# Fourteen more weight chunks by seven part products, with the sums and joins written anew

## The chip, the cores and the metric

One Trainium2 chip, one of its cores. The time is device microseconds of one execution of the whole program; several executions are timed and their median is given. A profile is one execution taken by the hardware profiler; its times are counted from the start of its span.

## The reference, cut to what matters

Four layers run on 256 tokens of width 1024, all in float32. The first two (the "first block") are a feed-forward part, a mixer and a second feed-forward part. The mixer multiplies the normed tokens by one wide matrix and splits the result:

```python
u = rms_norm(h, mix_norm[l])
(z_s, xbc, dt_s, qkv, z_d, b_d, a_d, gate_s, gate_d) = jnp.split(u @ w_in[l], split_points, axis=-1)
y_s = mamba2_branch(z_s, xbc, dt_s, ...)        # scan over 32 heads; y * silu(z), normed by groups
y_d = deltanet_branch(qkv, z_d, b_d, a_d, ...)  # qkv = silu(conv of 4 taps(qkv)), then q, k, v
merged = sigmoid(gate_s) * (y_s @ ssm_w_branch[l]) + sigmoid(gate_d) * (y_d @ dn_w_branch[l])
h = h + merged @ w_out[l]
```

The last two layers (the "second block") are a retention and convolution mixer, a cross attention, and a feed-forward part whose "up" product goes through a short convolution before it is gated.

## The kernel before, in words

**Chunks.** All weights stream from memory through a ring of three slots of 1 MB (`stream`, issued on SP's queue). A slot, a chunk, is 16 tiles of 128 x 128 and gives 256 output features for 256 tokens. A chunk c is loaded once chunk c - 2 has begun on TensorE (PE).

**Two ways to multiply a chunk.** Plain (`product`): 16 matmuls with 256 moving columns. By seven part products (`Tensor.seven`): the 2 x 2 blocks of the weights and of the tokens are combined by sums, as in Winograd's form of Strassen's algorithm, and seven products of half the size (4 matmuls of 128 columns each, 28 in all) replace eight. They are named B11, B21, B22, T1 to T4 and collect in two PSUM banks, X and Y. Four sums of weights are needed, made on VectorE (DVE) by `weights_by_dve` (for xbc's five chunks on GpSimd by `weights_by_pool`); four sums of tokens are made once for a stage (`sums_by_dve`, for the feed-forward outputs `feed_by_pool`). The order on PE, where the sums of tokens are old, is B11, B21, T4, then, once the first weight sums are there, T3, T2 (X is complete), T1, B22 (Y is complete). ScalarE (ACT) copies one quarter of X (`part_by_act`, L1006), and `join` on DVE adds the quarters into two tiles of output.

**Which chunks.** Every feed-forward chunk and many others go by seven. In the first block's mixer xbc has five of twelve (`BY_SEVEN`), z six of eight (`Z_SEVEN`) and q, k, v six of twelve, the odd ones (`Q_SEVEN`).

**The order around the change.** The scan of the first branch runs in 19 steps (`BESIDE`). Steps 0 to 6 carry the chunks z1 to z7, steps 7 to 18 the chunks q0 to q11. In a step PE multiplies the chunk, then makes the scan's y product (steps 0 to 15; it needs DVE's `mix` of that step), then spreads decays for three steps on. In steps 7, 11, 15 and 18 it also sums squares over partitions (`y_norm`), for which DVE must have added the squares (`y_summed`, at the end of steps 5, 9, 13 and 17). After step 18 come four z_d chunks and one gate chunk, all by seven.

DVE works through each step in a fixed order, and it takes no instruction out of turn: the weight sums of the **next** chunk if it goes by seven, the join of this chunk if it does, `mix` of the next step (L1705), the convolution of a q, k, v chunk (three taps for two tiles, L1616, once ACT has made the first tap, L1265 or L1279), `y_out` (L1712, L1714), for z chunks the gate (L1688), and in steps 5, 9, 13 and 17 the addition of squares (L1744, L1746). For a plain q, k, v chunk ACT copies the bank to the padded tile (L1273) and DVE has neither sums nor join.

**The start.** The tokens x come in four quarters on ACT's queue, behind the gain of the first norm; the first chunk's rows come in four pieces on SP's. The first two chunks are multiplied plain with raw tokens (`opening`). The second chunk is loaded once the last quarter of x has landed, and its load is one transfer; behind it on SP stand the constants, parameters and the third chunk.

Of the kernel before, what the change touches and what calls it, by code (L numbers as in the profile page):

```python
# [15 lines left out]
P = 128  # L16
# [128 lines left out]
class Sems:  # L145


    def __init__(self, ctx, nc):
# [137 lines left out]
class Lane:  # L286


    def __init__(self, e, sems, banks):
        self.e, self.sems, self.banks, self.seen = e, sems, banks, Seen()  # L290


class Tensor:
# [46 lines left out]
    def chunk(self):  # L340

        c, at = divmod(self.used, TILES)
        assert at == 0
        self.used += TILES
        if c:
            self.e.wait_ge(self.sems.w_loaded[c % RING], 16 * loads(c))
        self.fresh = c > 0
        return self.ring[:, c % RING, :]
# [39 lines left out]
    def seven(self, sums, f, at, X, Y, acts, first, last, ready=None, new=False, by_token=False):  # L388


        e, sems = self.e, self.sems
        if at[0] == 0:
            self.whole = self.chunk()
        a = lambda i, g: self.whole[:, (i * GROUPS + g) * P:(i * GROUPS + g + 1) * P]
        s = lambda i, g: sums.s[:, f % 2, i - 1, g * P:(g + 1) * P]
        part = lambda bank, i: bank[:, i * P:(i + 1) * P]

        def product(bank, i, weights, what, fresh, stop):
            for g in at:
                if ready:  # L400
                    ready(what, g)

                both = (acts(what, g), weights(g)) if by_token else (weights(g), acts(what, g))
                ins = self.mm(part(bank, i), *both, fresh and g == at[0], stop and g == at[-1])
            return ins

        def summed(n):
            e.wait_ge(sems.sum_by_pool if f in BY_POOL else sems.sum_by_dve, 4 * SUMMED[f] + n)

        def finished(ins):  # L410
            if last:
                ins.then_inc(sems.bulk_done, 1)

        product(X, 0, lambda g: a(0, g), "B11", first, False)
        product(X, 1, lambda g: a(1, g), "B21", False, False)
        if ready:
            summed(4)
            product(Y, 2, lambda g: s(4, g), "B22", first, False)
            if new:
                product(Y, 1, lambda g: s(1, g), "T1", False, False)  # L420
            product(X, 2, lambda g: s(2, g), "T2", False, False)
            finished(product(X, 3, lambda g: s(3, g), "T3", False, last))
            if not new:
                product(Y, 1, lambda g: s(1, g), "T1", False, False)
            finished(product(Y, 0, lambda g: a(3, g), "T4", False, last))
        else:
            product(Y, 0, lambda g: a(3, g), "T4", first, False)
            summed(2)
            product(X, 3, lambda g: s(3, g), "T3", False, False)
            summed(3)  # L430
            finished(product(X, 2, lambda g: s(2, g), "T2", False, last))
            product(Y, 1, lambda g: s(1, g), "T1", False, False)
            summed(4)
            finished(product(Y, 2, lambda g: s(4, g), "B22", False, last))

    def opening(self, outs, done, n, again=False):

# [7 lines left out]
        for at, (m, k) in enumerate(order):  # L445
            if at == SUM_AT[n] and n and not again:
                self.square_sums(n)
                if n == CLOSE1 + 1:
                    self.square_sums(CLOSE1)
            if m == 0 and not again:  # L450
                e.wait_ge(sems.raw_ready, scaled(n) + k + 1)
            if n == 0 and not again and m == 0 and k % 2 == 0:
                e.wait_ge(sems.rows_loaded[k // 2], 16)
            i = m * KD + k

            ins = self.mm(outs[m], w[:, i * P:(i + 1) * P], raw[:, k, :], k == 0 and (m == 0 or done[0]), k == KD - 1 and done[m])
            if k == KD - 1 and done[m]:
                ins.then_inc(sems.bulk_done, 1)
# [100 lines left out]
def stream(e, sems, parts, ring, before):  # L559

    c = 0
    for dram, n in parts:
        for i in range(n):
            before(c)
            if c >= RING:
                e.wait_ge(sems.w_used, c - RING + 1)

            if c:
                e.dma_start(ring[:, c % RING, :], dram[i]).then_inc(sems.w_loaded[c % RING], 16)
            c += 1  # L570

# [469 lines left out]
def last_weights_by_dve(v, seven, ring, f):  # L1041
# [2 lines left out]
    w = ring[:, c % RING, :].rearrange("p (i n) -> p i n", i=4)  # L1044
    s = seven.s[:, f % 2]
    e.wait_ge(sems.sum_by_dve, 4 * SUMMED[f] + 3)
    e.tensor_tensor(s[:, 3, :], w[:, 1, :], s[:, 1, :], ALU.subtract).then_inc(sems.sum_by_dve, 1)  # L1047


def weights_by_dve(v, seven, ring, f, last=True):  # L1050
# [5 lines left out]
    if f >= 2:  # L1056

        e.wait_ge(sems.w_used, FAST[f - 2] + 1)
    e.tensor_tensor(s[:, 0, :], w[:, 2, :], w[:, 3, :], ALU.add).then_inc(sems.sum_by_dve, 1)  # L1059
    e.tensor_tensor(s[:, 2, :], w[:, 0, :], w[:, 2, :], ALU.subtract).then_inc(sems.sum_by_dve, 1)  # L1060
    e.wait_ge(sems.sum_by_dve, 4 * SUMMED[f] + 1)
    e.tensor_tensor(s[:, 1, :], s[:, 0, :], w[:, 0, :], ALU.subtract).then_inc(sems.sum_by_dve, 1)  # L1062
    if last:
        last_weights_by_dve(v, seven, ring, f)

# [1 line left out]
def weights_by_pool(g, seven, ring, f):  # L1067
# [8 lines left out]
    e.tensor_tensor(s[:, 0, :], w[:, 2, :], w[:, 3, :], ALU.add).then_inc(sems.sum_by_pool, 1)
    e.tensor_tensor(s[:, 2, :], w[:, 0, :], w[:, 2, :], ALU.subtract).then_inc(sems.sum_by_pool, 1)
    e.wait_ge(sems.sum_by_pool, 4 * SUMMED[f] + 1)
    e.tensor_tensor(s[:, 1, :], s[:, 0, :], w[:, 0, :], ALU.subtract).then_inc(sems.sum_by_pool, 1)
# [10 lines left out]
def sums_by_dve(v, x, seven, at):  # L1090
# [5 lines left out]
    e.tensor_tensor(tx[1], high[:, :, P:S], tx[0], ALU.subtract).then_inc(sems.tx_by_dve, 1)  # L1096
    e.wait_ge(sems.tx_by_dve, at + 2)
    e.tensor_tensor(tx[2], high[:, :, P:S], low[:, :, P:S], ALU.subtract).then_inc(sems.tx_by_dve, 1)
    e.tensor_tensor(tx[3], high[:, :, 0:P], tx[1], ALU.subtract).then_inc(sems.tx_by_dve, 1)


def join(v, seven, L, name, i, high=None, in_place=False, to=None):
# [7 lines left out]
    twice = lambda x: x.unsqueeze(1).to_broadcast([P, 2, P])  # L1110
    e.wait_ge(sems.part_copied, PARTS_FROM[L, name] + i + 1)

    e.tensor_tensor(quarter[:, 0:2, 0, :], twice(a), X[:, 1:3, :], ALU.add).then_inc(sems.dve_step, 1)  # L1113
    e.wait_ge(sems.dve_step, seen.up("dve_step"))
    e.tensor_tensor(w, u, X[:, 3, :], ALU.add).then_inc(sems.bulk_read_dve, 1)  # L1115
    e.wait_ge(sems.bulk_done, BULK.filled(L, name, (i, 1)))
    e.tensor_tensor(quarter[:, 0, 1, :], u, Y[:, 1, :], ALU.add).then_inc(sems.dve_step, 1)  # L1117
    e.wait_ge(sems.bulk_read_dve, BULK.read(L, name, (i, 0)))
    if in_place:

        high = c[:, 1, :]
        e.wait_ge(sems.dve_step, seen["dve_step"] + 1)
# [78 lines left out]
def feed_by_pool(g, m, L, job):  # L1201
# [3 lines left out]
    def hidden(k):  # L1205
# [317 lines left out]
def first_dve(v, m, m2, L, par, par_next, cst, ring, ones):  # L1523
# [1405 lines left out]
def program(nc, hT_d, memT_d, pos_d, p1, w1, p2, w2, cst_d, dmask_d, outT):  # L2929
    with ExitStack() as ctx:  # L2930
# [30 lines left out]
        with nc.Block() as block:  # L2961
# [206 lines left out]
```

## Time and profile before

| | us |
|---|---|
| median of 3 runs | 3204.95 (3203.97 to 3206.16) |
| the profiled execution, its own time | 3207.67 |
| its span | 3205.9 |
| PE busy | 3187.9 (99%) |
| DVE busy | 2350.6 (73%) |
| ACT busy | 665.5 (21%) |
| GpSimd busy | 274.5 (9%) |

Busy time is the time in which an engine has at least one instruction in work; matmuls are pipelined, so a busy PE need not be at its peak. Instructions of one engine overlap a little: where one lasts 0.68 us, the next may begin 0.60 us after it. A float32 matmul of the program is two matmul records in the trace, so a chunk by seven is 56 records and a plain one 32.

### The profile page before, as it was taken

How to read it: one execution, taken by the hardware profiler on the slowest of the kernel's cores; microseconds unless marked ns; L12 is line 12 of the kernel's file. 1: busy time of each engine (PE TensorE's matmuls, PEld its weight loads, DVE VectorE, ACT ScalarE, POOL GpSimd, SP SyncE). 2: the span in 40 equal slices, each digit the busy share in tenths (PEclk: the TensorE clock that was granted, in tenths of full speed). 3: DMA queues.
4: the chain of work that ended last, by engine and by line, in shares of the span. 5: the costliest groups of instructions: out<-in, count | busy, mean ns of one | idle time of the engine just before them, and what ended most of it. 6: DMA issues, size and time to landing. Idle time of an engine off the chain costs nothing.

```text
span 3205.9 us, 59487 instructions
## 1 busy us (share of the span) xinstructions
PE 3187.9 (99%) x25008; PEld 3034.8 (95%) x25008; DVE 2350.6 (73%) x5234; ACT 665.5 (21%) x1625; POOL 274.5 (9%) x339
## 2 busy tenths in 40 slices
PE   9999999999999999999999999999999999999998
PEld 9999999899999999998999999879999999889998
DVE  6657786276676577873867898877786988877885
ACT  1113433211111134332211111211211111212211
POOL 0202000001102020000011000300021000300031
PEclk9999999999999999999999999999999999999999
DMA  5544444344444444443544444344444445343453
GB/s 203 171 158 136 141 146 154 103 162 169 170 170 165 157 141 145 148 149 110 193 165 167 168 166 168 130 148 145 149 169 170 161 169 172 120 156 130 160 172 132
DMA packets 89643, 497.50 MB, mean 155 GB/s; under 512 B 25088, under 2 KB 29600, under 8 KB 30368
## 3 DMA queue, kind: packets, MB, share of 16 engines
q1 hardware_dynamic: 70608, 489.45, 44.8%
q10 hardware_dynamic: 18768, 4.25, 0.7%
q8 instruction: 197, 3.23, 0.4%
q14 instruction: 70, 0.57, 0.0%
HBM read 491.55 MB, written 2.11 MB: 154 GB/s over the span
## 4 chain that ended last, share of the span: by engine, by line
PE 94%; DVE 4%; ACT 1%; issue 0%; DMA 0%; ACTq 0%; DVEq 0%
PE bank L352 87%; DVE arena L1062 1%; DVE arena L1047 1%; DVE arena L1060 1%; PE bank L2063 1%; PE bank L2858 0%; PE bank L2117 0%; PE bank L2802 0%; PE bank L2839 0%; DVE arena L1059 0%; ACT arena L2425 0%; PE bank L2042 0%; DVE arena L2697 0%; DVE arena L2704 0%; PE bank L523 0%
## 5 line engine op out<-in xcount | busy, mean ns | idle before, releaser
L352 PE MATMUL bank<-arena 128*128 128x128 f32 x9240 | 1092.8, 275 | 2.6 <-DVE arena L1047 2.6
L352 PEld LDWEIGHTS bank<-arena 128*128 128x128 f32 x9240 | 1061.6, 192 | 3.4 <-DVE arena L1047 3.4
L352 PE MATMUL bank<-arena,ring 128*128 128x128 f32 (+1 forms) x6312 | 991.1, 310 | 2.4 <-DMA ring<-w 1.3
L352 PEld LDWEIGHTS bank<-arena,ring 128*128 128x128 f32 x6312 | 896.0, 192 | 59.6 <-issue 2.9
L352 PE MATMUL bank<-xT,ring 128*128 128x128 f32 (+1 forms) x5008 | 725.2, 300 | 0.3 <-DVE arena L1127 0.3
L352 PEld LDWEIGHTS bank<-xT,ring 128*128 128x128 f32 x5008 | 669.8, 192 | 31.0 <-issue 0.7
L1006 ACT ACTIVATE arena<-bank 128x128 f32<-128x128 f32 x311 | 85.9, 276 | 1105.3 <-PE bank L352 1099.5
L1059 DVE TENSOR_TENSOR arena<-ring 128x512 f32<-128x512 f32 x343 | 235.2, 686 | 107.1 <-PE bank L352 103.8
L1113 DVE TENSOR_TENSOR arena<-arena,bank 128x256 f32<-128x256 f32 x311 | 129.6, 417 | 220.0 <-ACT arena L1006 219.0
L352 PE MATMUL bank<-xT,arena 128*128 128x128 f32 x1928 | 255.6, 276 | 0.1
L1047 DVE TENSOR_TENSOR arena<-ring,arena 128x512 f32<-128x512 f32 x343 | 241.9, 705 | 11.5
L1062 DVE TENSOR_TENSOR arena<-arena,ring 128x512 f32<-128x512 f32 x343 | 242.9, 708 | 0.0
L1060 DVE TENSOR_TENSOR arena<-ring 128x512 f32<-128x512 f32 x343 | 241.0, 703 | 0.0
L352 PEld LDWEIGHTS bank<-xT,arena 128*128 128x128 f32 x1928 | 234.8, 192 | 1.6 <-DVE arena L1047 1.6
L2479 DVE SCALAR_TENSOR_TENSOR arena<-arena,par 128x256 f32<-128x256 f32 x480 | 204.2, 494 | 0.0
L1117 DVE TENSOR_TENSOR arena<-arena,bank 128x128 f32<-128x128 f32 x311 | 88.5, 284 | 131.0 <-PE bank L352 130.7
L1616 DVE SCALAR_TENSOR_TENSOR arena<-arena,par 128x256 f32<-128x256 f32 x288 | 138.2, 548 | 50.3 <-ACT arena L1279 34.8
L1208 POOL TENSOR_TENSOR arena<-arena 128x128 f32<-128x128 f32 x66 | 40.1, 607 | 1161.0 <-DVE arena L1138 651.9
L1124 DVE TENSOR_TENSOR arena<-arena,bank 128x256 f32<-128x256 f32 x311 | 129.3, 416 | 10.6
L2732 POOL TENSOR_TENSOR arena<-arena 128x512 f32<-128x512 f32 x10 | 44.9, 4494 | 661.1 <-ACT arena L2344 661.0
L1115 DVE TENSOR_TENSOR arena<-arena,bank 128x128 f32<-128x128 f32 x311 | 89.2, 287 | 10.7
L1127 DVE TENSOR_TENSOR arena<-arena,bank 128x128 f32<-128x128 f32 x311 | 86.8, 279 | 0.0
(332 smaller groups left out, 2213.6 us busy)
## 6 DMA issues: line engine op xcount, KB each, us to landing
ring<-w SPq DMA_DIRECT2D x461, 1024.0 KB, 4.9
ring<-w SPq DMA_DIRECT2D x4, 256.0 KB, 5.6
hT<-hT_d ACTq DMA_DIRECT2D x4, 256.0 KB, 6.2
arena<-blocks_d ACTq DMA_DIRECT2D x4, 256.0 KB, 5.7
arena<-base_d ACTq DMA_DIRECT2D x16, 64.0 KB, 5.0
arena<-memT_d SPq DMA_DIRECT2D x1, 1024.0 KB, 9.1
outT<-hT SPq DMA_DIRECT2D x4, 256.0 KB, 2.5
arena<-dmask_d SPq DMA_DIRECT2D x1, 768.0 KB, 10.5
```

The source lines that it names most:

```text
L352: ins = self.e.matmul(out, lhsT, rhs, start=start, stop=stop)
L1047: e.tensor_tensor(s[:, 3, :], w[:, 1, :], s[:, 1, :], ALU.subtract).then_inc(sems.sum_by_dve, 1)
L1059: e.tensor_tensor(s[:, 0, :], w[:, 2, :], w[:, 3, :], ALU.add).then_inc(sems.sum_by_dve, 1)
L1060: e.tensor_tensor(s[:, 2, :], w[:, 0, :], w[:, 2, :], ALU.subtract).then_inc(sems.sum_by_dve, 1)
L1062: e.tensor_tensor(s[:, 1, :], s[:, 0, :], w[:, 0, :], ALU.subtract).then_inc(sems.sum_by_dve, 1)
L1113: e.tensor_tensor(quarter[:, 0:2, 0, :], twice(a), X[:, 1:3, :], ALU.add).then_inc(sems.dve_step, 1)
L1115: e.tensor_tensor(w, u, X[:, 3, :], ALU.add).then_inc(sems.bulk_read_dve, 1)
L1117: e.tensor_tensor(quarter[:, 0, 1, :], u, Y[:, 1, :], ALU.add).then_inc(sems.dve_step, 1)
L1124: e.tensor_tensor(last, twice(w), Y[:, 0:2, :], ALU.add).then_inc(sems.dve_step, 1)
L1127: e.tensor_tensor(quarter[:, 0, 1, :], quarter[:, 0, 1, :], Y[:, 2, :], ALU.add).then_inc(sems.bulk_read_dve, 1)
L1616: ins = stt(y, m.pad[:, n % 2, kk, tap:tap + S], col(w, 4 * tile + tap), y, ALU.mult, ALU.add)
L2479: ins = stt(y, x, w, y, ALU.mult, ALU.add)
```

## The change

The sums of weights and of tokens get other signs, so that one instruction makes two of the weight sums; the join has four instructions instead of five; T3 collects in Y instead of X. z4 and the six even q, k, v chunks of both layers of the first block go by seven. The second chunk's load is split in two halves with a semaphore each. The gain is loaded behind the first quarter of x.

```diff
-Z_SEVEN = (1, 2, 3, 5, 6, 7)
-Q_SEVEN = (1, 3, 5, 7, 9, 11)
+Z_SEVEN = (1, 2, 3, 4, 5, 6, 7)
+Q_SEVEN = tuple(range(12))
...
+SUM_OF = {3: 0, 1: 1, 2: 2, 4: 3}
...
 class Tensor: chunk
-        if c:
+        if c == 1:
+            self.e.wait_ge(self.sems.half_loaded, 16)
+        elif c:
             self.e.wait_ge(self.sems.w_loaded[c % RING], 16 * loads(c))
...
 seven, where the sums of tokens are old
             product(Y, 0, lambda g: a(3, g), "T4", first, False)
             summed(2)
-            product(X, 3, lambda g: s(3, g), "T3", False, False)
+            product(Y, 2, lambda g: s(3, g), "T3", False, False)
             summed(3)
             finished(product(X, 2, lambda g: s(2, g), "T2", False, last))
             product(Y, 1, lambda g: s(1, g), "T1", False, False)
             summed(4)
-            finished(product(Y, 2, lambda g: s(4, g), "B22", False, last))
+            finished(product(Y, 3, lambda g: s(4, g), "B22", False, last))
...
 opening
+            if n == 0 and again and (m, k) == (1, 0):
+                e.wait_ge(sems.w_loaded[1], 16)
...
 stream
-            if c:
+            if c == 1:
+                e.dma_start(ring[:, c, 0:SLOT // 2], dram[i][:, 0:SLOT // 2]).then_inc(sems.half_loaded, 16)
+                e.dma_start(ring[:, c, SLOT // 2:], dram[i][:, SLOT // 2:]).then_inc(sems.w_loaded[c], 16)
+            elif c:
                 e.dma_start(ring[:, c % RING, :], dram[i]).then_inc(sems.w_loaded[c % RING], 16)
...
 weights_by_dve (weights_by_pool alike), last_weights_by_dve
-    e.tensor_tensor(s[:, 0, :], w[:, 2, :], w[:, 3, :], ALU.add).then_inc(sems.sum_by_dve, 1)
-    e.tensor_tensor(s[:, 2, :], w[:, 0, :], w[:, 2, :], ALU.subtract).then_inc(sems.sum_by_dve, 1)
-    e.wait_ge(sems.sum_by_dve, 4 * SUMMED[f] + 1)
-    e.tensor_tensor(s[:, 1, :], s[:, 0, :], w[:, 0, :], ALU.subtract).then_inc(sems.sum_by_dve, 1)
+    e.tensor_tensor(s[:, 0:2, :], w[:, 2:3, :].to_broadcast([P, 2, GROUPS * P]), w[:, 0:4:3, :], ALU.add).then_inc(sems.sum_by_dve, 2)
+    e.wait_ge(sems.sum_by_dve, 4 * SUMMED[f] + 2)
+    e.tensor_tensor(s[:, 2, :], s[:, 1, :], w[:, 0, :], ALU.add).then_inc(sems.sum_by_dve, 1)
...
-    e.tensor_tensor(s[:, 3, :], w[:, 1, :], s[:, 1, :], ALU.subtract).then_inc(sems.sum_by_dve, 1)
+    e.tensor_tensor(s[:, 3, :], w[:, 1, :], s[:, 2, :], ALU.add).then_inc(sems.sum_by_dve, 1)
...
 join
-    e.tensor_tensor(quarter[:, 0:2, 0, :], twice(a), X[:, 1:3, :], ALU.add).then_inc(sems.dve_step, 1)
-    e.wait_ge(sems.dve_step, seen.up("dve_step"))
-    e.tensor_tensor(w, u, X[:, 3, :], ALU.add).then_inc(sems.bulk_read_dve, 1)
-    e.wait_ge(sems.bulk_done, BULK.filled(L, name, (i, 1)))
-    e.tensor_tensor(quarter[:, 0, 1, :], u, Y[:, 1, :], ALU.add).then_inc(sems.dve_step, 1)
-    e.wait_ge(sems.bulk_read_dve, BULK.read(L, name, (i, 0)))
...
-    e.tensor_tensor(last, twice(w), Y[:, 0:2, :], ALU.add).then_inc(sems.dve_step, 1)
-    seen.up("dve_step")
-    e.wait_ge(sems.dve_step, seen["dve_step"])
-    e.tensor_tensor(quarter[:, 0, 1, :], quarter[:, 0, 1, :], Y[:, 2, :], ALU.add).then_inc(sems.bulk_read_dve, 1)
+    e.tensor_tensor(quarter[:, 0:2, 0, :], twice(a), X[:, 1:3, :], ALU.add).then_inc(sems.bulk_read_dve, 1)
+    e.wait_ge(sems.bulk_done, BULK.filled(L, name, (i, 1)))
+    e.wait_ge(sems.bulk_read_dve, BULK.read(L, name, (i, 0)))
+    e.tensor_tensor(quarter[:, 0:2, 1, :], twice(u), Y[:, 1:3, :], ALU.subtract).then_inc(sems.dve_step, 1)
...
+    e.wait_ge(sems.dve_step, seen.up("dve_step"))
+    e.tensor_tensor(last, Y[:, 0:2, :], twice(w), ALU.subtract).then_inc(sems.dve_step, 1)
+    seen.up("dve_step")
+    e.tensor_tensor(quarter[:, 0, 1, :], quarter[:, 0, 1, :], Y[:, 3, :], ALU.add).then_inc(sems.bulk_read_dve, 1)
...
 first_dve, in the steps
+        if name == "z_s" and i == 7:
+            weights_by_dve(v, m.seven_q, ring, FAST_FROM[L, "q_7"])
...
 program, ACT's queue
-                e.dma_start(pars[0][:, 0:KD], p1[0][:, 0:KD]).then_inc(sems.gain_loaded, 16)
                 for i in range(4):
                     two = slice(2 * i, 2 * i + 2)
                     e.dma_start(hT[:, two, :], hT_d.rearrange("(k p) n -> p k n", p=P)[:, two, :]).then_inc(sems.h_loaded[i], 16)
+                    if i == 0:
+                        e.dma_start(pars[0][:, 0:KD], p1[0][:, 0:KD]).then_inc(sems.gain_loaded, 16)
```

The sums of tokens (`sums_by_dve`, and `feed_by_pool` on GpSimd) keep their four instructions each, with operands swapped and one subtraction turned into an addition.

## Rows read from the trace of the kernel before

**Rows 1.** The page's busy time, share of the span and instructions of each engine.
```profile
PE 3187.9 (99%) x25008; PEld 3034.8 (95%) x25008; DVE 2350.6 (73%) x5234; ACT 665.5 (21%) x1625; POOL 274.5 (9%) x339
```

**Rows 2.** Who PE waited for: us in total, times, longest.
```profile
PE bank L352 <- DVE arena L1047: 2.6, 4, 0.7
```

**Rows 3.** The chain that ended last: start us, us, work (x matmul records).
```profile
362.95 6.25 PE bank L352 x56
370.34 6.91 PE bank L352 x32
...
460.84 31.26 PE bank L352 x280
```

**Rows 4.** Stretches, first layer: start:end, length, engines' busy us, clock, DMA, GB/s.
```profile
317.98:370.34 52.36, 52.36 (x440) 48.33 (x439) 38.47 (x80) 24.49 (x57) 0.00 (x0) 1.00 0.42 142
370.34:460.84 90.50, 90.50 (x622) 80.64 (x622) 71.48 (x154) 33.09 (x76) 0.00 (x0) 1.00 0.41 140
460.84:492.10 31.26, 31.26 (x282) 31.26 (x282) 27.07 (x65) 16.14 (x32) 0.00 (x0) 1.00 0.50 169
```

**Rows 5.** DVE's timeline, chunk q1 into q3: start us, us, instruction.
```profile
385.49 0.42 DVE L1124 TENSOR_TENSOR arena<-arena,bank 128x256 f32<-128x256 f32 x1
385.83 0.28 DVE L1127 TENSOR_TENSOR arena<-arena,bank 128x128 f32<-128x128 f32 x1
386.03 0.95 DVE L1705 TENSOR_TENSOR arena<-arena 128x768 f32<-128x768 f32 x1
387.09 2.46 DVE L1616 SCALAR_TENSOR_TENSOR arena<-arena,par 128x256 f32<-128x256 f32 x6
389.47 0.47 DVE L1712 SCALAR_TENSOR_TENSOR arena<-arena,par,bank 128x256 f32<-128x256 f32 x1
...
390.32 0.68 DVE L1059 TENSOR_TENSOR arena<-ring 128x512 f32<-128x512 f32 x1
...
391.52 0.68 DVE L1062 TENSOR_TENSOR arena<-arena,ring 128x512 f32<-128x512 f32 x1
392.24 0.69 DVE L1047 TENSOR_TENSOR arena<-ring,arena 128x512 f32<-128x512 f32 x1
392.85 0.95 DVE L1705 TENSOR_TENSOR arena<-arena 128x768 f32<-128x768 f32 x1
...
397.73 0.69 DVE L1744 TENSOR_TENSOR arena<-arena 128x512 f32<-128x512 f32 x1
```

**Rows 6.** Groups by line and shape: busy us, mean ns, idle before.
```profile
L2585 DVE TENSOR_TENSOR arena<-arena 128x1024 f32<-128x1024 f32 x8 | 9.8, 1219 | 0.4 <-ACT arena L2356 0.4
```

**Rows 7.** Timeline of one step of "up", second half, second block's first layer.
```profile
2368.47 0.69 DVE L1059 TENSOR_TENSOR arena<-ring 128x512 f32<-128x512 f32 x1
2368.64 0.83 POOL L1208 TENSOR_TENSOR arena<-arena 128x128 f32<-128x128 f32 x1 [3.15 <-DVE arena L2704]
2369.08 0.94 DVE L1060 TENSOR_TENSOR arena<-ring 128x512 f32<-128x512 f32 x1
...
2370.91 0.83 DVE L1047 TENSOR_TENSOR arena<-ring,arena 128x512 f32<-128x512 f32 x1
...
2371.67 0.41 DVE L1113 TENSOR_TENSOR arena<-arena,bank 128x256 f32<-128x256 f32 x1
...
2372.84 0.28 DVE L1127 TENSOR_TENSOR arena<-arena,bank 128x128 f32<-128x128 f32 x1
...
2375.05 0.68 DVE L1059 TENSOR_TENSOR arena<-ring 128x512 f32<-128x512 f32 x1
```

**Rows 8.** Timeline of the start; in brackets idle before and its releaser.
```profile
15.90 7.17 PE L352 MATMUL bank<-arena,ring 128*128 128x256 f32 x32 [1.31 <-DMA ring<-w]
21.15 0.69 DVE L1059 TENSOR_TENSOR arena<-ring 128x512 f32<-128x512 f32 x1 [1.65 <-DMA ring<-w]
...
24.70 1.06 PE L352 MATMUL bank<-xT,arena 128*128 128x128 f32 x8
```

**Rows 9.** A stretch after the narrow products of the first layer; columns as rows 4.
```profile
234.00:240.00 6.00, 6.00 (x41) 6.00 (x40) 3.73 (x13) 2.36 (x5) 0.00 (x0) 0.72 0.52 175
```

More of the change, by code:

```diff
@@ L155, in __init__ @@
         self.w_loaded = [sem(f"w_loaded{i}") for i in range(RING)]
+        self.half_loaded = sem("half_loaded")
         self.w_used = sem("w_used")
@@ L394, in seven @@
         a = lambda i, g: self.whole[:, (i * GROUPS + g) * P:(i * GROUPS + g + 1) * P]
-        s = lambda i, g: sums.s[:, f % 2, i - 1, g * P:(g + 1) * P]
+        s = lambda i, g: sums.s[:, f % 2, SUM_OF[i], g * P:(g + 1) * P]
         part = lambda bank, i: bank[:, i * P:(i + 1) * P]
@@ L417, in seven @@
             summed(4)
-            product(Y, 2, lambda g: s(4, g), "B22", first, False)
+            product(Y, 3, lambda g: s(4, g), "B22", first, False)
             if new:
                 product(Y, 1, lambda g: s(1, g), "T1", False, False)
-            product(X, 2, lambda g: s(2, g), "T2", False, False)
-            finished(product(X, 3, lambda g: s(3, g), "T3", False, last))
+            finished(product(X, 2, lambda g: s(2, g), "T2", False, last))
+            product(Y, 2, lambda g: s(3, g), "T3", False, False)
             if not new:
@@ L428, in seven @@
             summed(2)
-            product(X, 3, lambda g: s(3, g), "T3", False, False)
+            product(Y, 2, lambda g: s(3, g), "T3", False, False)
             summed(3)
@@ L1075, in weights_by_pool @@
         e.wait_ge(sems.w_used, FAST[f - 2] + 1)
[L1076 to L1079, printed above, removed]
+    e.tensor_tensor(s[:, 0:2, :], w[:, 2:3, :].to_broadcast([P, 2, GROUPS * P]), w[:, 0:4:3, :], ALU.add).then_inc(sems.sum_by_pool, 2)
+    e.wait_ge(sems.sum_by_pool, 4 * SUMMED[f] + 2)
+    e.tensor_tensor(s[:, 2, :], s[:, 1, :], w[:, 0, :], ALU.add).then_inc(sems.sum_by_pool, 1)
     e.wait_ge(sems.sum_by_pool, 4 * SUMMED[f] + 3)
-    e.tensor_tensor(s[:, 3, :], w[:, 1, :], s[:, 1, :], ALU.subtract).then_inc(sems.sum_by_pool, 1)
+    e.tensor_tensor(s[:, 3, :], w[:, 1, :], s[:, 2, :], ALU.add).then_inc(sems.sum_by_pool, 1)
 def tokens_by_dve(v, m, seven, n, at):
@@ L1095, in sums_by_dve @@
     e.wait_ge(sems.tx_by_dve, at + 1)
-    e.tensor_tensor(tx[1], high[:, :, P:S], tx[0], ALU.subtract).then_inc(sems.tx_by_dve, 1)
+    e.tensor_tensor(tx[1], tx[0], high[:, :, P:S], ALU.subtract).then_inc(sems.tx_by_dve, 1)
     e.wait_ge(sems.tx_by_dve, at + 2)
-    e.tensor_tensor(tx[2], high[:, :, P:S], low[:, :, P:S], ALU.subtract).then_inc(sems.tx_by_dve, 1)
-    e.tensor_tensor(tx[3], high[:, :, 0:P], tx[1], ALU.subtract).then_inc(sems.tx_by_dve, 1)
+    e.tensor_tensor(tx[2], low[:, :, P:S], high[:, :, P:S], ALU.subtract).then_inc(sems.tx_by_dve, 1)
+    e.tensor_tensor(tx[3], high[:, :, 0:P], tx[1], ALU.add).then_inc(sems.tx_by_dve, 1)
 def join(v, seven, L, name, i, high=None, in_place=False, to=None):
@@ L1111, in join @@
     e.wait_ge(sems.part_copied, PARTS_FROM[L, name] + i + 1)
-    e.tensor_tensor(quarter[:, 0:2, 0, :], twice(a), X[:, 1:3, :], ALU.add).then_inc(sems.dve_step, 1)
-    e.wait_ge(sems.dve_step, seen.up("dve_step"))
-    e.tensor_tensor(w, u, X[:, 3, :], ALU.add).then_inc(sems.bulk_read_dve, 1)
+    e.tensor_tensor(quarter[:, 0:2, 0, :], twice(a), X[:, 1:3, :], ALU.add).then_inc(sems.bulk_read_dve, 1)
     e.wait_ge(sems.bulk_done, BULK.filled(L, name, (i, 1)))
-    e.tensor_tensor(quarter[:, 0, 1, :], u, Y[:, 1, :], ALU.add).then_inc(sems.dve_step, 1)
     e.wait_ge(sems.bulk_read_dve, BULK.read(L, name, (i, 0)))
+    e.tensor_tensor(quarter[:, 0:2, 1, :], twice(u), Y[:, 1:3, :], ALU.subtract).then_inc(sems.dve_step, 1)
     if in_place:
         high = c[:, 1, :]
-        e.wait_ge(sems.dve_step, seen["dve_step"] + 1)
     last = (seven.high[:, i % 2] if high is None else high).rearrange("p (t n) -> p t n", n=P)
-    e.tensor_tensor(last, twice(w), Y[:, 0:2, :], ALU.add).then_inc(sems.dve_step, 1)
+    e.wait_ge(sems.dve_step, seen.up("dve_step"))
+    e.tensor_tensor(last, Y[:, 0:2, :], twice(w), ALU.subtract).then_inc(sems.dve_step, 1)
     seen.up("dve_step")
-    e.wait_ge(sems.dve_step, seen["dve_step"])
-    e.tensor_tensor(quarter[:, 0, 1, :], quarter[:, 0, 1, :], Y[:, 2, :], ALU.add).then_inc(sems.bulk_read_dve, 1)
-    seen.up("dve_step")
+    e.tensor_tensor(quarter[:, 0, 1, :], quarter[:, 0, 1, :], Y[:, 3, :], ALU.add).then_inc(sems.bulk_read_dve, 1)
 def ffn_by_dve(v, L, job, m, ring, opened=False):
@@ L1209, in hidden @@
         e.wait_ge(sems.pool_step, g.seen.up("pool_step"))
-        e.tensor_tensor(th[2], high[:, P:S], low[:, P:S], ALU.subtract)
-        e.tensor_tensor(th[1], high[:, P:S], th[0], ALU.subtract).then_inc(sems.pool_step, 1)
+        e.tensor_tensor(th[2], low[:, P:S], high[:, P:S], ALU.subtract)
+        e.tensor_tensor(th[1], th[0], high[:, P:S], ALU.subtract).then_inc(sems.pool_step, 1)
         e.wait_ge(sems.pool_step, g.seen.up("pool_step"))
-        e.tensor_tensor(th[3], high[:, 0:P], th[1], ALU.subtract).then_inc(sems.th_ready, 1)
+        e.tensor_tensor(th[3], high[:, 0:P], th[1], ALU.add).then_inc(sems.th_ready, 1)
     for k in range(HALF):
```

## The prediction

> **What bounds the kernel now.** I read the page's busy times first. TensorE (PE) is busy 3187.9 us of 3205.9, VectorE (DVE) 2350.6 us [rows 1]. PE sets the time, and whatever shortens its queue counts in full as long as nobody else is late. Then the waits of PE: in the whole body it waits for DVE 2.6 us, in four places [rows 2]. So DVE hides behind PE nearly everywhere, but an average of 73% says nothing of a single stage. The next view is therefore the chain in order of time around the changed chunks. A chunk from seven products takes PE 6.25 us, a plain one 6.91 us, and a step of the scan (chunk, y product, decay spread) 7.39 us with seven, from 362.95 to 370.34 [rows 3]. Converting a chunk is worth 0.66 us of PE. The stretches come last: in the seven z steps DVE is busy 38.47 of 52.36 us, in the twelve q, k, v steps 71.48 of 90.50 us, and in the five chunks after them 27.07 of 31.26 us [rows 4]. In the q, k, v stretch DVE has only 19 us left. The second layer runs the same program, and the sums below count it twice.
>
> **Converted chunks: what PE saves.** One z and six q, k, v chunks in each of two layers: 14 x 0.66 = 9.2 us less PE work. Without a new wait the q, k, v stretch would be 90.50 - 6 x 0.66 = 86.5 us.
>
> **What DVE pays for one converted chunk.** The old sums are four additions over 512 elements; from 390.32 to the next instruction at 392.85 they take 2.53 us [rows 5]. In that run a new instruction starts 0.60 us after an independent one, and 0.72 after one it must wait for (391.52 to 392.24), 0.04 behind its end of 0.68. The new first sum is one instruction of 1024 elements, which the trace of before shows once, with a mean of 1219 ns [rows 6]. All the others depend on their forerunner: 1.22 + 0.04 + 0.72 + 0.61 = 2.59 us. So the sums are not cheaper: the second old sum stood in the shadow of the first one's end, and the new form exposes that end. Bounds for the wide one: 2 x 0.60 = 1.20 (two narrow ones back to back) to 2 x 0.68 = 1.36; I take 1.22, its own row. The join goes from five instructions to four over the same 896 elements, but the first three now form a chain: 0.46 + 0.46 + 0.34 + 0.20 = 1.46 us, with 0.42 + 0.04 behind a dependent 256-wide one, 0.34 and 0.20 behind independent ones [rows 5]. The old one takes 1.17 + 0.20 = 1.37 us where all its data lie ready [rows 7]. Subtracting and adding are the same kind of instruction here (0.68 both, L1059 and L1062), so the changed signs cost nothing. A converted chunk adds 2.59 + 1.46 = 4.05 us to DVE and takes nothing from it: the plain chunk's copy was ScalarE's.
>
> **The q, k, v stretch, step by step.** DVE does in each step the sums of the next chunk, the join, the mask product of the next step, the convolution, and y. From the mask product to the next sums is 386.03 to 390.32 = 4.29 us, in which the convolution starts 1.06 us after the mask product, since it waits for ScalarE's first tap; that pace stays without the mask product too [rows 5]. All steps being alike, DVE needs 4.29 + 2.59 + 1.46 = 8.34 us a step, PE 7.39. The stall is then a sum along DVE. Chunk q0 starts at 370.34 and ends at 376.59; join from its second half on 1.00, mask product to y 4.29: DVE is free at 381.9, at step 8. Steps 8 to 15 take 8 x 8.34 = 66.7, two of them with an addition of squares (397.73: 0.72 + 0.34 = 1.06 us each, 2.1): 450.7. Steps 16 and 17 have no y: 2.59 + 1.46 + 1.06 + 2.38 = 7.5 each: 465.7. Step 17 ends with the last addition of squares, 0.72 + 0.42, at 466.8; PE's product of these squares stands in its queue ahead of the next stretch and waits for it, and takes 0.43 us (6.91/16): the next stretch starts at 467.3 instead of 460.84. That is 6.5 us later, where PE alone would be 4.0 earlier. Before this last wait PE stalls too, at a chunk's fourth product, which needs the sums; these waits are inside the same sum. In the z steps 4.05 us more for DVE fit in its 13.9 us of idle time, so there the 0.66 us is kept. After the stretch DVE needs 27.07 us plus about a microsecond for 31.26, so its delay doesn't spread. Per layer +6.5 - 0.66 = +5.8; two layers **+11.6 us**. Bounds: 0.3 us a step either way (the wide sum, the join), 10 steps, 2 layers: 6 us.
>
> **The other sums and joins.** Where PE has slack the 0.06 and 0.09 us are hidden behind it. Not so in the second half of "up" in the second block: there a step takes 6.58 us (2368.47 to 2375.05) against PE's 6.25, and PE waits 1.3 us at its end in each layer [rows 2, 7]. GpSimd works beside DVE there. L1059 starts before GpSimd's instruction and keeps its 0.69 us; L1060, asked for while GpSimd runs, takes 0.94 [rows 7]. Read as taking turns, the wide sum runs untouched and one turn is saved: 1.22 + 0.04 + 0.94 + 0.04 + 0.83 - 0.07 = 3.00 us against 3.20 (2368.47 to 2371.67), join +0.09: 0.11 us a step, 1.2 in 11 steps, of a wait of 1.3. I take -1.0 a layer, **-2.0 us**. Read as a stretch by 0.94/0.68 of whatever runs beside GpSimd, it would be 3.47 us, +0.36 a step, +4 a layer. The bounds are -2.6 and +8; I take turns, since L1059 wasn't stretched. The Trainium skill, "SBUF — State Buffer", section "Who interferes with whom", says the same: the pair of ports that DVE and GpSimd share is an exclusive lock for the whole instruction, not a split of bandwidth. By that rule the sum is the -2.0; a split would give the +8.
>
> **The start.** PE waits 1.31 us for the second chunk's load and goes on at 15.90 [rows 8]. Half the load lands earlier, so most of that wait goes; what is late next is the third chunk: DVE's sums start on its landing at 21.15, and take 2.59; at 23.74 the product that needs all four can run, which now runs at 24.70 [rows 8]. That leaves 0.96; the second issue of the split load stands in SP's queue ahead of the constants, the parameters and this third chunk, so I take **-0.7 us** (bounds 0 and -1.3). The gain's load, moved behind the first quarter of x on ScalarE's queue, swaps the order of two issues whose landings are both needed for the first scaled tile: 0, by less than an issue either way. The last join stands on the path to the output: after its second bank it takes 0.46 + 0.34 + 0.28 instead of 0.20 + 0.34 + 0.28: **+0.3 us**.
>
> **Sum.** 11.6 - 2.0 - 0.7 + 0.3 = +9.2 us. The profiled execution took 3207.67 us (span 3205.9), so 3216.9; the median of the runs is 2.7 lower, 3204.95, so **3214.1 us**. No change, as far as this kernel can be measured, is within 0.2%, 6.4 us: 3198.5 to 3211.4.
>
> **Rivals.** *DVE keeps up* (faster): PE's 9.2 us are gained whole, and 3204.95 - 9.2 - 2.0 - 0.7 + 0.3 = 3193.4. It decides at 7.2 us of DVE a step; the 71.48 us of before plus 6 x 4.05 are 95.8, more than 86.5 even with no gap at all, and against it [rows 4]. It needs a wide sum or a join much below its rows. 0.09. *DVE's step is cheaper than charged* by 0.35 us (ends overlap better): 10 x 0.35 x 2 = 7 us back, 3207: 0.21. *The clock falls*: PE idles before the last product of squares: the sums of the last chunk are ready at 458.2 + 1.2, four of its seven products follow in 3.6, and from 463.0 to 466.8 nothing can run. After a stretch of narrow products the granted clock is 0.72 between 234 and 240, that is the lower level of 1.2 GHz for part of it, 6 x 0.28 = 1.7 us lost [rows 9]; at both places +3.4, 3217.5: 0.14. *GpSimd stretches the wide sum*: +8 for -2, 3224: 0.05. The forecast has 0.51. Its own range is 3208 to 3220; with the rivals until 2 in 10 are left out 3205 to 3221. Slower by over 0.2%: most of the forecast (0.48), the clock and GpSimd: 0.67. Within: 0.24. Faster: 0.09.
>
> **What would show it.** In the profile after: no plain chunk between z1 and the d stretch but z0's; that stretch at about 97 us in both layers with DVE busy some 95; waits of PE for the sums at a chunk's fourth product and one of about 4 us at the product of squares in step 18; a DVE step of 8.3 us; the wide sum at 1.22; four waits at the end of "up" near zero; the wait of 1.31 us gone. A stretch below 90 us makes the prediction wrong; a join under 1.2 or a wide sum under 0.9 us would be why.

## The result and the profile after

| us | before | after |
|---|---|---|
| median of five runs | 3204.97 (3203.97 to 3207.29) | 3221.56 (3219.96 to 3223.22) |
| span of the profiled execution | 3205.9 | 3218.2 |

The ratio is 1.0053, with a 95% interval of 1.0042 to 1.0064: slower by 16.6 us. Slower was the forecast, but by 9.2 us, and 3221.56 lies 0.6 above the range. The profile is of the fastest of the five runs, so each term is read from its own place below and not from the two spans.

The page's busy times, as [rows 1]: PE is busy 5.9 us less than before, and the time grows all the same.

```profile
PE 3182.0 (99%) x25344; PEld 3040.6 (94%) x25344; DVE 2379.7 (74%) x4678; ACT 660.9 (21%) x1627; POOL 278.5 (9%) x329
```

Whom PE waited for (us, times, longest), to be read against [rows 2]. Two waits are new: for the wide sum (L1070), and one in each layer for the last addition of squares (L1753), 3.7 us in the first layer and 3.4 in the second. Of the five waits for L1058, 0.6 us lie at the start; the other four, 2.5 us, are those at the end of "up".

```profile
PE bank L358 <- DVE arena L1070: 8.9, 7, 1.9
PE bank L2079 <- DVE arena L1753: 7.1, 2, 3.7
PE bank L358 <- DVE arena L1058: 3.1, 5, 1.0
```

The three stretches of [rows 4], with the same columns: z got its 0.66 us (52.36 to 51.70). The twelve q, k, v chunks take 98.09 us instead of 90.50, with DVE busy 90.69 of them. The five chunks behind take 32.68 instead of 31.26, at a mean clock of 0.96 where it was 1.00.

```profile
316.99:368.69 51.70, 51.70 (x464) 48.66 (x464) 43.63 (x79) 24.66 (x57) 0.00 (x0) 1.00 0.42 143
368.69:466.78 98.09, 88.56 (x765) 83.19 (x765) 90.69 (x181) 31.12 (x76) 0.00 (x0) 1.00 0.38 129
466.78:499.46 32.68, 32.68 (x282) 32.68 (x282) 27.60 (x55) 16.17 (x32) 0.00 (x0) 0.96 0.47 162
```

One step of DVE in that stretch (start, us, instruction; compare [rows 5]). From wide sum to wide sum it is 8.39 us, and no instruction in it has a bracket with a wait: DVE runs without rest. The sums take 2.59 us (398.11 to 400.70), the join 1.51 (to 402.21), mask product to y the rest.

```profile
398.11 1.22 DVE L1070 TENSOR_TENSOR arena<-ring 128x1024 f32<-128x1024 f32 x1
399.36 0.69 DVE L1072 TENSOR_TENSOR arena<-arena,ring 128x512 f32<-128x512 f32 x1
400.09 0.69 DVE L1058 TENSOR_TENSOR arena<-ring,arena 128x512 f32<-128x512 f32 x1
400.70 0.41 DVE L1122 TENSOR_TENSOR arena<-arena,bank 128x256 f32<-128x256 f32 x1
401.21 0.42 DVE L1125 TENSOR_TENSOR arena<-arena,bank 128x256 f32<-128x256 f32 x1
401.67 0.42 DVE L1131 TENSOR_TENSOR arena<-bank,arena 128x256 f32<-128x256 f32 x1
402.01 0.28 DVE L1133 TENSOR_TENSOR arena<-arena,bank 128x128 f32<-128x128 f32 x1
402.21 0.95 DVE L1710 TENSOR_TENSOR arena<-arena 128x768 f32<-128x768 f32 x1
...
406.50 1.22 DVE L1070 TENSOR_TENSOR arena<-ring 128x1024 f32<-128x1024 f32 x1
```

PE's timeline at the end of the stretch (in brackets the idle time before and its releaser). The squares' product takes 0.89 us and the next 16 records 3.41, where the same 16 take 1.95 with the wait filled (busy_pe, below): behind the wait PE runs at the lower of its two clocks (granted clock 0.50 from 466.57 to 469.57). The last two lines are the same place in the second layer.

```profile
461.11 1.06 PE L358 MATMUL bank<-xT,arena 128*128 128x128 f32 x8
465.89 0.89 PE L2079 MATMUL bank<-arena,cst 128*128 128x256 f32 x2 [3.72 <-DVE arena L1753]
466.57 3.41 PE L358 MATMUL bank<-xT,ring 128*128 128x128 f32 x16
...
1354.06 1.19 PE L2079 MATMUL bank<-arena,cst 128*128 128x256 f32 x2 [3.38 <-DVE arena L1753]
1355.05 2.92 PE L358 MATMUL bank<-xT,ring 128*128 128x128 f32 x16
```

### The profile page after: what moved, and what is told of

Read it like the earlier page. It is cut to its first block, busy times and chain, and to the rows that moved or that the text cites. A ratio compares the mean times of both kernels' runs of the same rounds, so it can differ in the third digit from the quotient of the medians.

```text
span 3218.2 us, 59843 instructions
## 1 busy us (share of the span) xinstructions
PE 3182.0 (99%) x25344; PEld 3040.6 (94%) x25344; DVE 2379.7 (74%) x4678; ACT 660.9 (21%) x1627; POOL 278.5 (9%) x329
## 4 chain that ended last, share of the span: by engine, by line
PE 84%; DVE 13%; ACT 2%; issue 1%; DMA 1%; ACTq 0%; DVEq 0%; SPq 0%
PE bank L358 78%; DVE arena L1070 2%; DVE arena L1621 2%; DVE arena L1058 2%; DVE arena L1072 2%; DVE arena L1125 1%; ACT arena L2432 1%; DVE arena L1131 1%; DVE arena L2704 1%; DVE arena L1122 1%; DVE arena L2711 1%; PE bank L2865 0%; PE bank L2124 0%; PE bank L2809 0%; PE bank L2846 0%
## 5 line engine op out<-in xcount | busy, mean ns | idle before, releaser
L358 PE MATMUL bank<-arena 128*128 128x128 f32 x9576 | 1134.9, 275 | 11.4 <-DVE arena L1070 8.9
L358 PEld LDWEIGHTS bank<-arena 128*128 128x128 f32 x9576 | 1101.7, 192 | 13.5 <-DVE arena L1070 10.2
L358 PE MATMUL bank<-xT,ring 128*128 128x128 f32 (+1 forms) x4784 | 654.7, 291 | 0.0
L358 PEld LDWEIGHTS bank<-xT,ring 128*128 128x128 f32 x4784 | 613.0, 192 | 19.9 <-issue 0.9
L1070 DVE TENSOR_TENSOR arena<-ring 128x1024 f32<-128x1024 f32 x357 | 437.4, 1225 | 103.1 <-PE bank L358 96.8
L358 PE MATMUL bank<-xT,arena 128*128 128x128 f32 x2040 | 270.4, 275 | 0.7 <-DVE arena L1058 0.6
L1058 DVE TENSOR_TENSOR arena<-ring,arena 128x512 f32<-128x512 f32 x357 | 251.1, 703 | 11.8
L1131 DVE TENSOR_TENSOR arena<-bank,arena 128x256 f32<-128x256 f32 x325 | 137.9, 424 | 11.1
L1133 DVE TENSOR_TENSOR arena<-arena,bank 128x128 f32<-128x128 f32 x325 | 90.1, 277 | 0.0
L1048 ACT ACTIVATE arena<-arena 128x256 f32<-128x256 f32 x88 | 36.8, 418 | 251.4 <-DVE arena L1133 228.2
L890 ACT ACTIVATE xT<-hT 128x256 f32<-128x256 f32 x96 | 38.6, 412 | 173.8 <-DVE hT L1171 74.9
```

The costliest lines, as they stand in the source:

```text
L358: ins = self.e.matmul(out, lhsT, rhs, start=start, stop=stop)
L1058: e.tensor_tensor(s[:, 3, :], w[:, 1, :], s[:, 2, :], ALU.add).then_inc(sems.sum_by_dve, 1)
L1070: e.tensor_tensor(s[:, 0:2, :], w[:, 2:3, :].to_broadcast([P, 2, GROUPS * P]), w[:, 0:4:3, :], ALU.add).then_inc(sems.sum_by_dve, 2)
L1131: e.tensor_tensor(last, Y[:, 0:2, :], twice(w), ALU.subtract).then_inc(sems.dve_step, 1)
```

## The experiments

The theory after the two traces: VectorE's load makes the loss, the clock falls because PE stands still at the squares, and two small gains of the prediction ("up" and the start) didn't come. Its rivals were the new forms of the sums and joins, something else about even chunks by seven (banks, ScalarE, loads), and a clock that falls on its own. Twelve runs follow; each ratio is against the kernel before on the same chip.

**Which part of the change costs: q_six, q_twelve_old_forms, forms_only**

```diff
 q_six: from the kernel after
-Q_SEVEN = tuple(range(12))
+Q_SEVEN = (1, 3, 5, 7, 9, 11)
...
 q_twelve_old_forms: from the kernel before, the other way round
 forms_only: from the kernel after, Q_SEVEN and Z_SEVEN of before,
   one load for the second chunk, the gain first
```

> The changed kernel with the six even q, k, v chunks plain again; z4 by seven, the new sums and joins and the new start stay. Theory (VectorE is the bound in the q, k, v steps, since each converted even chunk gives it some 4.1 us more and TensorE only 0.66 us less): the stretch from q0 to the next one falls back from 98.1 to about 90.5 us, the five chunks behind it to 31.3, and the whole to 3203 to 3206 us, the kernel before. Rival (the new sums and joins themselves cost the time, everywhere they are used): it stays above 3212.

> The kernel before with nothing changed but all twelve q, k, v chunks by seven, in its old sums and joins. Theory (VectorE's load decides, the form hardly matters): a step of VectorE is 4.29 + 2.53 + 1.57 = 8.39 us, the stretch takes 97 to 98.5 us and the whole is about 17 to 18 us above the kernel before, 3222 to 3223. Rival (the dependent chain of the new forms makes the loss): a stretch of 91 us or less, and at most 3210 us.

> The kernel before with the new sums and joins alone: z4 and the even q, k, v chunks plain, the second load whole and the gain first, as before. Theory: nearly nothing, 3204.5 to 3205.5; the wide sum and the join cost VectorE 0.06 and 0.14 us a step where TensorE has slack, the up stage gains some 0.3 us in two layers, the last join costs 0.3. Rival (the forms cost): 3210 or more. Second rival (the up stage gains its whole 2 us): 3203.

Measured against the kernel before on the same chip (3203.77): q_six 3203.07, ratio 0.9997 (0.9988 to 1.0005); q_twelve_old_forms 3221.89, 1.0057 (1.0044 to 1.0069); forms_only 3204.72, 1.0004 (0.9995 to 1.0012). With six the stretch is 90.50 us in the first layer and 90.51 in the second, with twelve in the old forms 98.43. So the six even chunks make the loss in either form, and the forms by themselves can't be told from nothing. That rival is out.

**What holds the even chunks: one_tap**

```diff
-        for tap in range(3):
+        taps = 3 if name == "xbc" else 1
+        for tap in range(taps):
...
```

> The changed kernel in which VectorE adds one tap instead of three in the convolution of q, k, v (two taps are left out, so q, k, v are not the reference's). Theory (only VectorE's time in a step makes the loss): its step falls by four instructions of 0.40 us from 8.39 to 6.8 us, under TensorE's 7.39; the stretch of the twelve chunks goes from 98.1 to 86.5 to 87.5 us, the wait for the squares goes, and the whole is 12 x 0.66 us under the kernel with six, some 8 us under the kernel before. Rival (the even chunks are held by something else: banks, ScalarE's copy, the loads): the stretch stays above 92 us and the whole above the kernel before.

3195.70 us, ratio 0.9972 (0.9961 to 0.9983). The chain of waits shows the twelve chunks from 370.09 to 456.66:

```profile
370.09 6.25 PE bank L358 x56
...
456.66 31.26 PE bank L358 x280
```

That is 86.57 us, against 86.5 from twelve chunks at PE's own pace. Banks, copies and loads are the same as in the kernel after; with less work for DVE alone PE waits for nothing there. The lost time is DVE's.

**The clock: busy_pe and idle_only.** One fills PE's wait, the other makes the wait without the twelve chunks.

```diff
 busy_pe: from the kernel after, on PE ahead of the wait for the squares
+            if p == STEPS - 1:
+                for _ in range(14):
+                    e.matmul(bank[:, 0:P], const("ones"), const("ones"), start=True, stop=True)
 idle_only: from q_six, on VectorE ahead of the addition of squares
+            if p == 17:
+                s = m.seg[:, 0:3]
+                for _ in range(2):
+                    tt(s, s, s, ALU.max)...
```

> The changed kernel with 14 products of ones with ones, some 3.1 us, put on TensorE in step 18 of the scan between the last q, k, v chunk and the wait for the last addition of squares; they write a bank that the next product overwrites. Theory (the clock falls to 1.2 GHz behind that wait of 3.7 us because TensorE stood still in it): the half-clock stretch of 3.4 us behind the wait goes in both layers, 1.7 us each, so about 3.4 us less than the changed kernel, 3218; the stretch to the squares keeps its length, the five chunks behind it go from 32.7 and 32.2 to 31.3. Rival (the clock falls for another reason): no change, 3221.6.

> The changed kernel with six q, k, v chunks by seven, in which VectorE does two idle instructions of some 2.6 us (2304 elements, on a buffer that is free by then) before the last addition of squares: TensorE gets a wait of about 4.1 us at the product of the squares, with nothing else of the twelve chunks. Theory (the standing still makes the clock fall): behind the wait a stretch at 1.2 GHz of about 3.4 us in both layers, 1.7 us lost in each; 2 x (4.1 + 1.7) = 11.6 us more than the kernel before. Rival (the clock falls for another reason, such as the twelve chunks): full clock behind the wait, 8.2 us more.

busy_pe: 3216.99, ratio 1.0042 (1.0029 to 1.0056), that is 3.5 us less than the kernel after by the two ratios. The intervals overlap, so here the traces decide. The chain of waits of the kernel after, q0 and the stretch behind the squares in both layers:

```profile
368.69 6.25 PE bank L358 x56
...
466.78 32.68 PE bank L358 x280
...
1256.86 6.25 PE bank L358 x56
...
1355.26 32.20 PE bank L358 x280
```

and that of busy_pe:

```profile
368.88 6.25 PE bank L358 x56
...
466.67 31.27 PE bank L358 x280
...
1255.33 6.27 PE bank L358 x56
...
1353.11 31.26 PE bank L358 x280
```

The twelve chunks take 98.09 and 98.40 us with the standing still and 97.79 and 97.78 without, the five behind them 32.68 and 32.20 against 31.27 and 31.26: 1.7 and 1.6 us, **3.3 us** of clock. PE's timeline there in busy_pe:

```profile
462.52 3.29 PE L2080 MATMUL bank<-cst 128*128 128x128 f32 x28
465.97 0.70 PE L2082 MATMUL bank<-arena,cst 128*128 128x256 f32 x2 [0.16 <-DVE arena L1753]
466.50 1.95 PE L358 MATMUL bank<-xT,ring 128*128 128x128 f32 x16
```

The 14 products make nothing that is used. (Another stretch at the lower clock, at 1340 us in the kernel after and at 452 in busy_pe, lies among the waits for the sums, where DVE sets the pace and a slower PE costs little.)

idle_only: 3214.94 us, 1.0033 (1.0021 to 1.0045), 11.0 above the kernel before on the same chip, where 11.6 was expected for wait and clock and 8.2 for the wait alone. Its PE timeline, and its window behind the wait (columns as [rows 4]; the granted clock is the 0.50):

```profile
462.65 1.19 PE L2082 MATMUL bank<-arena,cst 128*128 128x256 f32 x2 [4.00 <-DVE arena L1756]
463.63 3.62 PE L358 MATMUL bank<-xT,ring 128*128 128x128 f32 x16
```

```profile
463.00:467.00 4.00, 4.00 (x18) 3.82 (x18) 3.40 (x7) 0.36 (x1) 0.00 (x0) 0.50 0.43 119
```

Standing still for 4.0 us is enough, with six chunks too. The price of such a fall is not fixed: in the ten places of this kind (two layers of the kernel after, q_twelve_old_forms, idle_only, gain_first and one_load) the five chunks behind the wait take 32.2 to 33.7 us instead of 31.3, that is 0.9 to 2.4 us more, 1.6 on average, and the product of squares itself 0.1 to 0.5 more. The clock that falls on its own is out at this place.

**A version between, and the stage "up": q_nine and nine_split**

```diff
 q_nine: from the kernel after, with one second load and the gain first
-Q_SEVEN = tuple(range(12))
+Q_SEVEN = (0, 1, 2, 3, 5, 6, 7, 9, 11)
 nine_split: the same, and in the join
-    e.tensor_tensor(quarter[:, 0:2, 1, :], twice(u), Y[:, 1:3, :], ALU.subtract)...
+    e.tensor_tensor(w, u, Y[:, 2, :], ALU.subtract)...
+    e.tensor_tensor(quarter[:, 0, 1, :], u, Y[:, 1, :], ALU.subtract)...
```

> Nine of the twelve q, k, v chunks by seven (4, 8 and 10 plain), z4 by seven, new sums and joins, the start as before. Theory (a step with a plain chunk gives VectorE back 8.05 - 4.3 = 3.7 us, which is enough for three steps of one us too much): no wait of TensorE for the sums in the q, k, v steps, 4 chunks x 0.66 us a layer, 5 us under the kernel before. Rival (each even chunk by seven costs 1.5 us, the mean of what six of them cost, 8.9 us): 3 x 1.5 x 2 - 1.3 = 8 us above.

> The kernel with nine, and the second instruction of the join split in its two halves of 128, the one that the next instruction needs first: the chain of three dependent instructions is gone, five instructions in some 1.39 us instead of four in 1.51. Theory for the up stage (the new join's 0.14 us kept VectorE from catching up in its first half, and so the four waits at its end stayed): a step of its first half 5.99 us instead of 6.11, of its second 6.26 instead of 6.38, the four waits of together 2 to 2.5 us near zero; 2 to 2.5 us under the kernel with nine. Rival (those waits have another cause): as the kernel with nine.

q_nine: 3199.41, ratio 0.9985 (0.9977 to 0.9994); its stretch is 88.54 us (369.75 to 458.29), 90.50 less three times 0.66. nine_split: 3195.84, ratio 0.9975 (0.9964 to 0.9986). For whom PE waited at the end of "up", in q_nine and then in nine_split (us, times, longest):

```profile
PE bank L355 <- DVE arena L1050: 2.1, 4, 0.6
```

```profile
PE bank L355 <- DVE arena L1050: 0.4, 1, 0.4
```

Four waits of 2.1 us became one of 0.4, by half the means that were expected: the join took 1.45 us and not 1.39, the steps of "up" 6.05 and 6.32 us and not 5.99 and 6.26. That 1.7 is the part of the 3.6 us between the medians that the traces place; in another 1.6 the two profiles differ by a stretch at the lower clock at 232 to 240 us, which q_nine's execution has and the other has not. The intervals of the two ratios overlap, but six of nine_split's seven executions lie below all eleven of q_nine.

**The start: gain_first, one_load, nine_halves, nine_split_again**

```diff
 gain_first: from the kernel after
+                e.dma_start(pars[0][:, 0:KD], p1[0][:, 0:KD])...   (ahead of the four quarters of x)
 one_load: from the kernel after, the second chunk in one load
 nine_halves: nine_split with the second load in two halves
 nine_split_again: nine_split once more
```

> The changed kernel with the gain's load first on ScalarE's queue again; the second load stays in two halves. Theory (ScalarE loads its function table only after it has the gain, and with the gain behind the first quarter of x that load no longer hides in the wait for x): the table load at 4.4 us instead of 5.2 to 6.3, the first product of the start at 6.6 instead of 7.1 to 8.1, no wait of TensorE for the second chunk, the products after the first layer's opening stages at 231.0 to 231.2 instead of 231.5 to 232.0. Rival (the first product is late because of the split load or by chance): it stays at 7.1 or later.

> The changed kernel with the second chunk in one load again; the gain stays behind the first quarter of x. Theory: the first product stays at 7.1 or later, TensorE waits for the second chunk again by 0.5 to 1.4 us, the third chunk's load is issued a microsecond earlier, and the products after the opening stages start at 231.6 to 232.2. Rival (the split load alone makes the start late): 231.2 and the first product at 6.6.

> The kernel with nine and the split join, and the second load in two halves, the gain first. Theory (the halves are worth what of the wait for the second chunk isn't taken over by the third one's sums): wait for the second chunk gone, 0 to 0.4 us under the kernel with nine and the split join, which is less than these runs can tell apart. Rival (a transfer that is ahead by half its length gives its whole wait): 1.1 us.

> The kernel with nine and the split join once more, beside the one with the halves: 0.25% under the kernel before, as before, the waits at the end of up near zero.

The first two were executed once each (3223.0 and 3221.3 us). ScalarE's timeline at the start, in the kernel after and then in gain_first:

```profile
1.59 0.46 ACTq L3007 DMA_DIRECT2D hT<-hT_d  x1
2.08 0.48 ACTq L3009 DMA_DIRECT2D par<-p  x1
2.60 1.75 ACTq L3007 DMA_DIRECT2D hT<-hT_d  x3
5.45 1.28 ACT L872 ACT_TABLE_LOAD   x1 [5.45 <-DMA par<-p]
6.74 0.91 ACT L876 ACTIVATE arena<-hT,par 128x256 f32<-128x256 f32 x2
```

```profile
4.38 1.28 ACT L872 ACT_TABLE_LOAD   x1 [4.38 <-issue]
6.01 0.91 ACT L876 ACTIVATE arena<-hT,par 128x256 f32<-128x256 f32 x2 [0.35 <-DMA hT<-hT_d]
```

The table load stands behind the wait for the gain. With the gain first it is over before x lands; behind the first quarter it is not, and PE's first product starts at 7.30 instead of 6.57. That is as expected for gain_first and, on this point, for one_load (7.15). But one_load missed: PE had no wait for the second chunk, because the first one ended only at 17.20, by slow landings of x, and its small products start at 232.80. gain_first's start at 231.33, where 231.0 to 231.2 was expected, and PE still waits 0.47 us there for the first half of the second chunk; in nine_halves, too, it waits 0.6 us where none was expected. With the gain first the small products start at 231.18, 231.11, 232.13, 231.18, 231.22 and 231.54 in six profiles with one load (mean 231.39), and at 231.33 and 231.12 with halves; with gain and halves both as changed at 231.74, 231.97, 231.93, 231.52 and 231.63 (mean 231.76). A microsecond of scatter between executions of one start lies over all of it, so the halves' worth stays open below 0.5 us. nine_halves 3196.03, 0.9974 (0.9964 to 0.9985), and nine_split_again 3195.86, 0.9973 (0.9962 to 0.9985), say the same. The version with nine and the split join is faster than both kernels, than the kernel before by 0.25% in one measurement and 0.27% in another.

## Why the prediction was wrong in size

| term, us | predicted | measured | from |
|---|---|---|---|
| twelve chunks at DVE's pace, two layers | +13.0 | +14.6 | 97.79 and 97.78 in busy_pe, less 90.50 |
| z4, two layers | -1.3 | -1.3 | the stretch of 51.70 |
| clock behind the squares | 0 | +3.3 | kernel after against busy_pe |
| up | -2.0 | -0.1 to -0.5 | the four waits at its end: 2.6 before, 2.5 after, 2.1 in forms_only |
| start | -0.7 | +0.4 | the means above |
| end | +0.3 | +0.3 | from PE's last 32 records to DVE's last group: 7.64 before (3192.62 to 3200.26), 7.90 after (3204.66 to 3212.56) |
| sum | +9.2 (rounded) | some +17 | the medians say +16.6 |

**DVE as the bound: right.** The path was the forecast one: DVE full, waits at the fourth product, one of "about 4 us" at the squares, measured as 3.7 and 3.4. The step was 8.39 for 8.34: the join's second instruction starts 0.51 us behind the first and not 0.46 (400.70 to 401.21; the code has two waits between them, and one where 0.46 was read), so the join takes 1.51. Ten steps of 0.05 a layer are 1.0 of the 1.6 us missing here. (The 2.6 us that the text started from as all of PE's waits for DVE are those for the weight sums alone: PE also waits 1.9 us for `ones` at the start and 1.8 us in the second block, the same in both kernels, so no term hangs on it.)

**The clock: the step that failed most.** The text saw the wait ("from 463.0 to 466.8 nothing can run") and priced the fall at 1.7 a layer from [rows 9], 3.4 in all; measured 3.3. But it stood as a rival at 0.14, and the sum put it at nothing without a reason. That the price came so close is in part luck: it was read at another place, and such falls cost 0.9 to 2.4 us behind the wait in the other profiles. It is no accident to be given a chance: all four profiles with the twelve chunks and this wait unfilled have it in both layers, and idle_only makes it at will.

**Up: turns were right, the stage gained nothing.** GpSimd beside DVE in the second half (start, us, instruction; compare [rows 7]):

```profile
2375.86 1.22 DVE L1070 TENSOR_TENSOR arena<-ring 128x1024 f32<-128x1024 f32 x1
2377.11 0.83 DVE L1072 TENSOR_TENSOR arena<-arena,ring 128x512 f32<-128x512 f32 x1
2377.97 0.83 DVE L1058 TENSOR_TENSOR arena<-ring,arena 128x512 f32<-128x512 f32 x1
2378.73 0.41 DVE L1122 TENSOR_TENSOR arena<-arena,bank 128x256 f32<-128x256 f32 x1
...
2382.24 1.22 DVE L1070 TENSOR_TENSOR arena<-ring 128x1024 f32<-128x1024 f32 x1
```

```profile
2376.02 1.37 POOL L1213 TENSOR_TENSOR arena<-arena 128x128 f32<-128x128 f32 x1 [228.09 <-DVE arena L2711]
```

The wide sum keeps its 1.22 us and GpSimd's first instruction takes 1.37 instead of 0.83: in both kernels it ends 0.31 us behind the DVE instruction that started ahead of it (2369.47 behind 2369.16 before, 2377.39 behind 2377.08 after). The Trainium skill, "SBUF — State Buffer", section "Who interferes with whom", has the shared ports as a lock for a whole instruction, and the trace agrees. The sums fell from 3.20 to 2.87 us and the step from 6.58 to 6.38. What failed is "where PE has slack the 0.06 and 0.09 us are hidden behind it". In the first half DVE starts late and catches up. The kernel before does so at 5.92 us a step, and its last step there waits for PE:

```profile
2296.39 0.68 DVE L1059 TENSOR_TENSOR arena<-ring 128x512 f32<-128x512 f32 x1
...
2302.30 0.68 DVE L1059 TENSOR_TENSOR arena<-ring 128x512 f32<-128x512 f32 x1
...
2359.16 0.29 DVE L1117 TENSOR_TENSOR arena<-arena,bank 128x128 f32<-128x128 f32 x1 [0.25 <-PE bank L352]
```

The kernel after needs 6.11 (0.05 more for the sums, 0.14 for the join). Both begin the first half 0.3 us behind PE's product of the step. Where GpSimd starts, DVE's sums were 3.3 us ahead of that product before (2361.90 against 2365.21) and are 1.4 ahead after (2375.86 against 2377.29); at the end of the stage both are some 0.5 ahead, which is too little for the last chunks. The first two lines are from the kernel before, the third from the kernel after:

```profile
2361.90 0.68 DVE L1059 TENSOR_TENSOR arena<-ring 128x512 f32<-128x512 f32 x1
2365.21 1.95 PE L352 MATMUL bank<-xT,ring 128*128 128x128 f32 x16
...
2377.29 1.95 PE L358 MATMUL bank<-xT,ring 128*128 128x128 f32 x16
```

What the second half gained, the first had lost. nine_split enters 2.2 us ahead (2352.95 against 2355.12), ends 1.6 ahead, and loses the waits.

**Start:** "0, by less than an issue either way" for the gain left out what stands behind it on ScalarE, the table load of 1.28 us: by the means it cost some 0.5 us (231.76 against 231.23 with the gain first and the halves kept). The halves, charged at -0.7, came to some -0.2 (231.23 against 231.39), which is within the scatter.

The range failed with these: its upper bound took the clock in, but not together with the two gains that didn't come. The time lies only 0.6 us above it.

## What to carry to other kernels

Count what a cheaper form on the bottleneck costs the engine beside it per step, and convert only as many as that engine can carry: nine of twelve gained 0.15% where twelve lost 0.53%. Where a forecast has PE standing still for microseconds, the price of the lower clock belongs in the sum, and filler products in the wait can save it (3.3 us here by the traces). A slack in which a late engine catches up is no free cover: ask whether it is caught up at the end.

## What the runs showed that was not expected

- PE that stood still for 3.4 to 4.0 us came back at the lower clock (0.50 in a window of idle_only): the next 16 records of a chunk took 2.9 to 3.6 us instead of 1.95, in all ten places. With 28 records of products nobody needs in the wait, the same 16 took 1.95 (granted clock 1.00).
- The lower clock also came behind a shorter wait, at one place and not at another: in the kernel after, PE stood still for 1.87 us ahead of both 450.79 and 1338.96, and the 24 records behind took 2.94 us (granted clock 1.00) and 4.55 us (0.63 from 1339 to 1343).
- Splitting one 256-wide instruction of DVE into two of 128 was faster where the next depended on it: the join took 1.45 us in five instructions and 1.51 in four.
- ScalarE's table load waits in order behind a DMA wait, and cost 0.7 us at the first product when it lost its cover.
- Profiles differ by short stretches at the lower clock where PE's work is the same: that of before has them at 232 to 240 and 580 to 592 us, that of forms_only at neither place. What starts these was not tried.
